# A hybrid encoder step on one core: the sample tile routed first, its rows gathered and dotted from step 7 on, all scatters behind

## What is computed

```
q = (xb @ w_pq).reshape(T, 8, 2, 128)
s = einsum('thcd,ckd->thck', q, sub_keys)
s1, i1 = top_k(s[:, :, 0], 16);  s2, i2 = top_k(s[:, :, 1], 16)
cand = s1[..., :, None] + s2[..., None, :]          # 256 a head
best, sel = top_k(cand, 16);  eidx = i1[sel] * 128 + i2[sel]
g = softmax(best)
a = gelu(einsum('thkd,td->thk', u_tab[eidx], xb))
y = h + einsum('thk,thkd->td', g * a, v_tab[eidx])
```

## Time and profile before

| | |
|---|---|
| median of 3 runs | 2551.08 us (2545.3 to 2557.47) |
| profiled execution | 2548.08 us, span of its instructions 2546.5 us |
| PE busy | 2267.8 us (89%) |
| PEld busy | 2012.0 us (79%) |
| DVE busy | 1816.8 us (71%) |
| POOL busy | 1141.8 us (45%) |
| ACT busy | 938.2 us (37%) |
| mean granted TensorE clock | 0.957 of full speed |
| moved by DMA | 722.70 MB, mean 284 GB/s |

### The profile page before, as it was taken

One profiled execution on the slowest core, in us unless ns is written; L12 is line 12 of the kernel. 1 busy time (PEld: TensorE's weight loads), 2 busy tenths in 40 slices (PEclk: granted clock), 3 DMA queues, 4 the chain that ended last, 5 costly groups with the idle time before them and its releaser, 6 DMA issues.

```text
span 2546.5 us, 36629 instructions
## 1 busy us (share of the span) xinstructions
PE 2267.8 (89%) x13843; PEld 2012.0 (79%) x13843; DVE 1816.8 (71%) x2242; ACT 938.2 (37%) x1030; POOL 1141.8 (45%) x618
## 2 busy tenths in 40 slices
PE   7989999999999992588878878879999999999998
PEld 5878777788999992588877878879887877777777
DVE  3555544554478991699876767677688988898988
ACT  5354543532433440233322223223433333333332
POOL 1020100120007887743787887884344544544441
PEclk9999999999999996799989998889999999999999
DMA  5453544496335673799999999999999999999997
GB/s 192 125 190 117 177 130 145 137 339 244 125 116 133 186 206 68 222 361 381 367 320 330 323 329 316 318 330 358 359 412 412 412 413 412 413 411 413 411 412 283
DMA packets 221520, 722.70 MB, mean 284 GB/s; under 512 B 55672, under 2 KB 105624, under 8 KB 154871
## 3 DMA queue, kind: packets, MB, share of 16 engines
q1 hardware_dynamic: 113872, 380.68, 40.3%
q0 software_dynamic: 87408, 318.89, 35.4%
q10 hardware_dynamic: 20151, 22.05, 2.5%
HBM read 679.70 MB, written 41.83 MB: 283 GB/s over the span
## 4 chain that ended last, share of the span: by engine, by line
PE 28%; POOL 25%; DMA 21%; DVE 15%; issue 9%; ACT 1%; SPq 1%; DVEq 0%; ACTq 0%; POOLq 0%
POOL g_dense L477 20%; PE banks L1329 8%; PE banks L1331 8%; PE banks L1330 8%; DMA v_raw<-in_v_tab 8%; DMA a_tile<-a_dense 7%; POOL u_row L471 6%; DVE h L1273 5%; DMA g_dense<-route,route_place 3%; DVE v_lo L1279 2%; DVE ring_lo L1279 1%; DVE u_lo L1194 1%; DMA a_dense<-gelu_out 1%; DVE u_row L1233 1%; DMA u_row<-in_u_tab,route_place 1%
## 5 line engine op out<-in xcount | busy, mean ns | idle before, releaser
L477 POOL DMA_INDIRECT g_dense<-route,route_place x256 | 536.4, 2095 | 302.0 <-DVE route_place L1187 176.7
L1331 PE MATMUL banks<-xT_hi,u_lo 128*128 128x256 f32 x2048 | 596.8, 291 | 0.0
L514 POOL DMA_INDIRECT v_row<-in_v_tab,route_place x128 | 339.4, 2652 | 410.6 <-DVE h L1273 365.3
L1233 DVE CUSTOM_DVE_ANT_0 u_row<-u_row,x_rows 128x2048 f32<-128x2048 f32 x128 | 292.7, 2291 | 236.3 <-DMA u_row<-in_u_tab,route_place 234.8
L1329 PE MATMUL banks<-xT_hi,ring_hi 128*128 128x256 f32 (+1 forms) x1280 | 386.7, 302 | 72.4 <-DVE u_lo L1194 72.2
L1329 PE MATMUL banks<-xT_hi,ring_lo 128*128 128x256 f32 x1024 | 302.8, 296 | 126.4 <-DVE u_lo L1194 126.3
L1331 PEld LDWEIGHTS banks<-xT_hi,u_lo 128*128 128x128 f32 x2048 | 410.4, 200 | 0.0
L1330 PE MATMUL banks<-xT_lo,ring_hi 128*128 128x256 f32 (+1 forms) x1280 | 383.7, 300 | 0.0
L853 DVE TENSOR_TENSOR ring_lo<-raw,ring_hi 128x2048 fp32r<-128x2048 f32 x72 | 165.0, 2291 | 215.3 <-ACT ring_hi L541 207.8
L1329 PEld LDWEIGHTS banks<-xT_hi,ring_hi 128*128 128x128 f32 x1280 | 253.0, 198 | 75.9 <-issue 75.9
L1329 PEld LDWEIGHTS banks<-xT_hi,ring_lo 128*128 128x128 f32 x1024 | 206.2, 201 | 131.4 <-issue 131.3
(11 more groups left out here) (256 smaller groups left out, 4826.9 us busy)
## 6 DMA issues: line engine op xcount, KB each, us to landing
v_raw<-in_v_tab SPq DMA_DIRECT2D x128, 1024.0 KB, 14.7
u_raw<-in_u_turned SPq DMA_DIRECT2D x64, 1024.0 KB, 6.8
raw<-in_u_turned SPq DMA_DIRECT2D x64, 1024.0 KB, 5.8
raw<-in_w_in SPq DMA_DIRECT2D x160, 256.0 KB, 3.4
raw<-in_w_out SPq DMA_DIRECT2D x64, 256.0 KB, 4.3
g_dense<-zeros POOLq DMA_DIRECT2D x16, 1024.0 KB, 28.3
raw<-in_w_pq SPq DMA_DIRECT2D x64, 256.0 KB, 3.6
a_dense<-gelu_out ACTq DMA_DIRECT2D x128, 128.0 KB
```

The costliest lines, as they stand in the source:

```text
L477: pool.indirect_dma_start(out=places, out_offset=bass.IndirectOffsetOnAxis(ap=routeU[:, t, 2, j:j + 1], axis=0), in_=route[:, t, 0, j:j + ...
L514: pool.indirect_dma_start(out=vrow[k % NVB][:, :], out_offset=None, in_=rows, in_offset=bass.IndirectOffsetOnAxis(ap=routeU[:, NT - 1, 1, ...
L1233: V.tensor_tensor_reduce(row[:, :], row[:, :], xrow[:, :], 1.0, 0.0, ALU.mult, ALU.add, adot[:, i:i + 1]).then_inc(dot_done, 1)
L1331: return MM(out, l1, h2, start=False, stop=last)
```

## The change

The sample tile is now the one that is routed by quarters, in the same places. The whole-tile routing of steps 13 to 25 is that of prompt tile 0; tile 1 stays in steps 26 to 50. Dots run from step 7 to step 124. POOL first waits for the last sweep over the scores (a new semaphore, raised at the end of step 4's sweep), then gathers the first 24 rows, and then issues all 256 scatters, with a gather behind scatters 0 and 2 of every five. There are five row buffers instead of three; the two new ones take the second halves of the rings in which the high parts of steps 2 and 3 of four lay, and these high parts move into the sample columns of the transposed activations, with a stride of 384 elements between runs of 128.

```diff
-SAMPLES = 13
-DOTS_FROM = SAMPLES + N_PARTS
+PROMPTS = 13
-LAST_DOT = 124
-NUB = 3
+FIRST_DOT, LAST_DOT = 7, 124
+NUB = 5
-APART = 104
...
-    if SAMPLES <= m < DOTS_FROM:
-        return NT - 1, m - SAMPLES
-    i = m - DOTS_FROM
+    if PROMPTS <= m < PROMPTS + N_PARTS:
+        return 0, m - PROMPTS
+    i = m - PROMPTS - N_PARTS
...
-    return min(DOTS, max(m + 1 - DOTS_FROM, 0) * DOTS // (LAST_DOT - DOTS_FROM))
+    return min(DOTS, max(m + 1 - FIRST_DOT, 0) * DOTS // (LAST_DOT - FIRST_DOT))
...
-        uH = [ringH[:, 0, :], ringL[:, 0, :], ringH[:, 1, :], ringL[:, 1, :]]
+        uH = [ringH[:, 0, :].rearrange("p (b e) -> p b e", e=P), ringL[:, 0, :].rearrange("p (b e) -> p b e", e=P),
+              xTh[:, :, TU:T], xTl[:, :, TU:T]]
...
-        urow = [at(f"u_row{i}", MX + 8 * i, [P, D]) for i in range(NUB)]
+        urow = [at(f"u_row{i}", kb, [P, D]) for i, kb in enumerate((MX, MX + 8, MX + 16, 56, 72))]
...
+            pool.wait_ge(swept, 1)
             gathered = 0
-            for j in range(SLOTS):
-                if j % (2 * TOPK) == 0:
-                    pool.wait_ge(rt_ready, 1 + j // (2 * TOPK))
+            while gathered < dots_after(PROMPTS + N_PARTS - 1) + NUB - 1:
+                if gathered % (2 * TOPK) == 0:
+                    pool.wait_ge(rt_ready, 1 + gathered // (2 * TOPK))
+                gather_dot(gathered)
+                gathered += 1
+            for j in range(N_SCATTER):
+                t, i = divmod(j, SLOTS)
+                if i == 0:
+                    pool.wait_ge(rt_ready, QUARTERS + 1 + t)
                 if j % TOPK == 0 and j:
                     pool.wait_ge(g_scat, 16 * j)
-                scatter(0, j)
-                if j == APART:
-                    pool.wait_ge(rt_ready, QUARTERS + 1)
-                if j >= APART and j % 2 == 0:
+                scatter(t, i)
+                if gathered < DOTS and j % 5 in (0, 2):
                     gather_dot(gathered)
                     gathered += 1
-            while gathered < dots_after(DOTS_FROM + 2 * N_PARTS) + NUB - 1:
-                gather_dot(gathered)
-                gathered += 1
-            pool.wait_ge(rt_ready, ROUTED)
-            for j in range(SLOTS):
-                if gathered < DOTS and j % 3 < 2:
-                    gather_dot(gathered)
-                    gathered += 1
-                if j % TOPK == 0:
-                    pool.wait_ge(g_scat, 16 * (SLOTS + j))
-                scatter(1, j)
             while gathered < DOTS:
                 gather_dot(gathered)
                 gathered += 1
...
-                A(uH[m % UR], rawu[m % UR], ACT.Copy).then_inc(u_hi_done, 1)
+                A(uH[m % UR], rawu[m % UR].rearrange("p (b e) -> p b e", e=P), ACT.Copy).then_inc(u_hi_done, 1)
...
-                    best_weights(QUARTERS + (NT - 1 - tile_part(m - 1)[0]), slice(0, PH))
+                    best_weights(QUARTERS + tile_part(m - 1)[0], slice(0, PH))
...
                 if m < N_SWEEPS:
                     sweep(3 * N_SWEEPS + m)
+                if m == N_SWEEPS - 1:
+                    dve.sem_inc(swept, 1)
```

In `routing_quarter` the tile index 0 becomes NT - 1, and its last instructions write the row number of the expert instead of the place in `g_dense`:

```diff
-                    V.scalar_tensor_tensor(out=place, in0=i2, scalar=float(P), in1=i1, op0=ALU.mult, op1=ALU.add)
-                    drain()
-                    V.tensor_scalar(routeU[:, 0:1, 2, places].rearrange("p o x -> p (o x)"), place, cst[:, C_AD + NT:C_AD + NT + 1],
-                                    cst[:, C_AD:C_AD + 1], ALU.mult, ALU.add).then_inc(rt_ready, 1)
+                    V.scalar_tensor_tensor(out=routeU[:, NT - 1:NT, 1, places].rearrange("p o x -> p (o x)"), in0=i1, scalar=float(P),
+                                           in1=i2, op0=ALU.mult, op1=ALU.add).then_inc(rt_ready, 1)
```

More of the change, by code:

```diff
@@ L295, in hybrid_layer @@
         row_used = sem("row_used")
+        swept = sem("scores_swept")
         urow_in = [sem(f"urow_in{i}") for i in range(NUB)]
@@ L1117, in routing_part @@
                     route_index(t, 1, 2)
-                    dve.wait_ge(best_exp, QUARTERS + NT - t)
+                    dve.wait_ge(best_exp, QUARTERS + 1 + t)
                     V.tensor_reduce(bst[:, 0, :], bv[:, :, :], AX.X, ALU.add)
@@ L1142, in routing_quarter @@
                 if j == 0:
-                    V.tensor_copy(tf[:, 4 * nb:4 * nb + 4, :], ti[:, 0, 4 * nb:4 * nb + 4, :])
+                    V.tensor_copy(tf[:, 4 * nb:4 * nb + 4, :], ti[:, NT - 1, 4 * nb:4 * nb + 4, :])
                     V.tensor_tensor(cand4[:, :, :].rearrange("p h (a b) -> p h a b", a=TOPK),
-                                    tvh[:, 0, heads, 0, :].unsqueeze(3).broadcast_to(few),
-                                    tvh[:, 0, heads, 1:2, :].broadcast_to(few), ALU.add)
+                                    tvh[:, NT - 1, heads, 0, :].unsqueeze(3).broadcast_to(few),
+                                    tvh[:, NT - 1, heads, 1:2, :].broadcast_to(few), ALU.add)
                     drain()
@@ L1172, in routing_quarter @@
                     drain()
-                    V.tensor_reduce(route[:, 0:1, 1 + c, places].rearrange("p o (h k) -> p (o h) k", h=2), eq4[:, :, :, :], AX.X, ALU.add)
+                    V.tensor_reduce(route[:, NT - 1:NT, 1 + c, places].rearrange("p o (h k) -> p (o h) k", h=2), eq4[:, :, :, :], AX.X, ALU.add)
                 else:
@@ L1179, in routing_quarter @@
                     drain()
-                    V.tensor_tensor(route[:, 0:1, 0, places].rearrange("p o (h k) -> p (o h) k", h=2), bv[:, heads, :],
+                    V.tensor_tensor(route[:, NT - 1:NT, 0, places].rearrange("p o (h k) -> p (o h) k", h=2), bv[:, heads, :],
                                     bst[:, 1, heads].unsqueeze(2).broadcast_to([P, 2, TOPK]), ALU.mult)
-                    i1 = route[:, 0:1, 1, places].rearrange("p o x -> p (o x)")
-                    i2 = route[:, 0:1, 2, places].rearrange("p o x -> p (o x)")
-                    place = bhf[:, 0, heads, :].rearrange("p h k -> p (h k)")
-                    V.scalar_tensor_tensor(out=place, in0=i2, scalar=float(P), in1=i1, op0=ALU.mult, op1=ALU.add)
-                    drain()
-                    V.tensor_scalar(routeU[:, 0:1, 2, places].rearrange("p o x -> p (o x)"), place, cst[:, C_AD + NT:C_AD + NT + 1],
-                                    cst[:, C_AD:C_AD + 1], ALU.mult, ALU.add).then_inc(rt_ready, 1)
+                    i1 = route[:, NT - 1:NT, 1, places].rearrange("p o x -> p (o x)")
+                    i2 = route[:, NT - 1:NT, 2, places].rearrange("p o x -> p (o x)")
+                    V.scalar_tensor_tensor(out=routeU[:, NT - 1:NT, 1, places].rearrange("p o x -> p (o x)"), in0=i1, scalar=float(P),
+                                           in1=i2, op0=ALU.mult, op1=ALU.add).then_inc(rt_ready, 1)
                 drain()
@@ L1193, in u_lo @@
                 dve.wait_ge(u_hi_done, m + 1)
-                V.tensor_tensor(uL[m % UR], rawu[m % UR], uH[m % UR].bitcast(F32), ALU.subtract).then_inc(u_lo_done, 1)
+                V.tensor_tensor(uL[m % UR].rearrange("p (b e) -> p b e", e=P), rawu[m % UR].rearrange("p (b e) -> p b e", e=P),
+                                uH[m % UR].bitcast(F32), ALU.subtract).then_inc(u_lo_done, 1)
             for s in range(16):
@@ L1584, in u_step @@
                     c = slice(b * P, (b + 1) * P)
-                    last = three(bank[q][:, 0:TU], uH[q][:, c], uL[q][:, c], xTh[:, b, 0:TU], xTl[:, b, 0:TU], b == 0, b == KC - 1)
+                    last = three(bank[q][:, 0:TU], uH[q][:, b, :], uL[q][:, c], xTh[:, b, 0:TU], xTl[:, b, 0:TU], b == 0, b == KC - 1)
                 last.then_inc(u_used, 1)
```

## The result

The changed kernel takes 2651.24 us (median of 4 runs, 2645.7 to 2662.94) against 2550.39 us before: 1.040 times as long, 95% interval 1.035 to 1.045. The profiled execution took 2647.4 us, its span is 2645.8 us.

A forecast was written before the change was run, and what follows sets the result against it. POOL's in-order queue after step 25 was taken as the bound: 620 us scatters, 177 gathers and 64 checks make 861 from 997, moving the V sweep by +101; added to the median 2551.1, that gives 2652 us, range 2582 to 2730.

The forecast's parts named there:

- The end of step 25: U sweep, steps 7 to 25: 20 early dots add 47.4 us to VectorE, moving the end from 957.8 to 997.
- The queue: POOL after step 25: 256 scatters 620 us, 104 gathers 177, 15 checks 64, in sum 861 us.
- A scatter: POOL after step 25: 2.12 us each plus 0.30 issue, 620 us for 256.
- A gather: POOL after step 25: 1.40 us each, 1.70 with issue, 177 us for 104.
- the filled stretch: Kernel before, 1226.8 to 1739.7 us, tile 1's scatters between gathers: POOL completely filled; source of prices for the forecast.
- The checks: POOL's 15 waits for earlier scatters after step 25: 4.3 us each, 64 us in sum.
- The last leg: Last gather's start to the V sweep's first matmul: 41.8 us, taken as unchanged.
- The V sweep's start: End of U sweep: last gather begins at 1857 instead of 1756, so the V sweep moves by +101 us.
- The surcharge: Time added to POOL's 1.55 us scatter: about 1.07 us times the time share of VectorE's two-input instructions.
- A: Rival after step 25: POOL mostly undisturbed, queue 646 us, DMA and VectorE bound instead, 2444 us; chance 0.09.
- B: Rival, U sweep from 997: TensorE mostly at 1.2 GHz, 10.2 us a step, 2790 us; chance 0.04.
- C: Rival in POOL's queue: checks wait behind queued gathers, 13 us each instead of 4.3, +130, 2780 us; chance 0.05.

The follow-up runs named there:

- one-input dot: Changed kernel with VectorE's dot replaced by a plain sum over the gathered row, the multiplication with the tokens left out: 2569.0 us.
- the best order of the work: Kernel before with gathers from scatter 80, tile 1 routed each step from 26 to 38, five gathers for six scatters: 2495.7 us, 0.977.
- both together: Kernel before with gathers from scatter 80, tile 1 routed each step, five gathers for six scatters, and tokens in PSUM: 2428.1 us, 0.951.

## Why the prediction was right

**The bound.** The prediction took POOL's in-order queue after step 25 as what sets the V sweep's start. It does: POOL is full from 995.2 to 1861.6, and taking half of its scatters away moved the V sweep by 232 us, while the buffers moved nothing.

**Its terms.** The end of step 25: 997 forecast, 994.9 measured for the routing, with 19 dots before it (the twentieth starts right behind it, and the first scatter does not wait for that). The queue: 861 forecast, 867 measured, from terms that were off in both directions. A scatter took 2.15 us and not 2.12, +8 us for 256, less 3 of issue. A gather took 1.57 and not 1.40, +18 us for 104: a gather's surcharge did not fall with VectorE's share. Fewer gathers began in a two-input instruction (61 of 104, where 63 of 86 had in the filled stretch before), but with 1.11 us of it left instead of 0.87. The checks cost 48 and not 64 us, −16: the price came from the filled stretch, with 0.67 gathers a scatter, and I had written that it was the dearer one. The last leg, from the last gather to the V sweep's first matmul, was 36.8 and not 41.8 us: 2 us less up to the end of dot 127 and 3 us less behind it. Why is open; the prediction had taken it as unchanged. The V sweep's start: 1899 forecast (1797.8 + 101), 1897.1 measured. That 2652 meets 2651 to a microsecond is luck in the signs of these, since single terms were up to 18 us off. That it lies near is not: the queue, its start and the way it was added up were right.

**The surcharge.** 1.07 us times the share of VectorE's two-input instructions was read from two stretches. The changed kernel has 98 `u_lo`, 107 dots and five two-input instructions of tile 1's routing in 867 us, 55%, and a surcharge of 0.60 (factor 1.09). With half of the scatters (96 `u_lo`, 105 dots and those five, 471 of 623 us, 76%) it was 0.92 and not 0.81, and with the one-input dot (98 `u_lo` and those five, 235 of 786 us, 30%) 0.37 and not 0.32. The rule holds near the shares from which it was taken, and gives somewhat too little away from them. The timelines say where it falls short:

| kernel | scatters | begun in a two-input instruction | us of it left, mean | mean scatter, us |
|---|---|---|---|---|
| changed | 256 | 137 (54%) | 1.23 | 2.15 |
| half of the scatters | 128 | 100 (78%) | 1.28 | 2.47 |
| one-input dot | 256 | 79 (31%) | 1.30 | 1.92 |

The share of scatters that VectorE holds up is its share of the time, within 2 points. One that is held up pays what is left less 0.12 us, which is 1.11 to 1.18 and not 1.07. Why more was left in the two experiments is open.

The prediction quotes the rule as one in which whoever starts first keeps the lock for the whole instruction, and says that the trace agrees. The traces show one half of that, a scatter behind VectorE. The other half they do not show: 35 scatters of the changed kernel were under way when a two-input instruction began, and it took its 2.29 us. The forecast used the first half only.

**What was priced at nothing.** The V sweep (748.7 us in both), the strided high parts (ScalarE's copy 1.91 us and `u_lo` 2.28 in the long stretch, as before) and the row buffers (shown by the run with three of them) were nothing.

**The rivals.** A, cheap POOL, needed scatters under 1.73 us; they took 2.15. That VectorE's two-input instructions make the surcharge is shown by the runs with a one-input dot, where a scatter took 1.92 and 1.89 us. It is not the whole loss: with the tokens in PSUM in both kernels the order still costs 69 of 101 us. B, TensorE's clock: the granted clock fell to 0.87 in the stretch, but the steps followed POOL at 867/98 = 8.8 us, where the prediction reckons 10.2 for the lower level. C, checks of 13 us: 13 of the 15 waited at all, the longest 9.05 us, and 48 us in sum are less than the 64 forecast.

## What to carry to other kernels

An in-order queue that looks 45% busy over the span can be the path for a third of it: find the stretch where busy, issue and waits of one engine add up to the stretch, and count what a change adds to the queue behind its last release. Work that one engine does cheaply while another stands is not waiting to be won; before filling a stand, look who uses it. Where GpSimd issues many indirect DMAs beside VectorE, an operand of VectorE's long instructions put in PSUM was worth as much (2.2% on the kernel before) as the best order of the work (2.3%), and both together were worth 4.9%.

## What was not expected of the hardware

The dots' part of the surcharge on POOL could be bought off with one copy: a dot whose second input lies in PSUM runs at the same 2.29 us and lets a scatter through at 1.57 us. A rival had been that reading PSUM makes the dot longer; it does not here. And the mean price of a scatter is a mixture of two: 1.56 us for one that begins outside VectorE's two-input instructions, what is left of the instruction and 1.43 us for one that begins inside. That gives 1.60 us in the stand, 2.15 in the changed kernel and 2.47 with half the scatters, for the same 128 numbers. Of the two engines only POOL pays: it is the start of the scatter that counts, and a two-input instruction that begins a moment later holds nobody up.
